# Two adaLN vectors and half a gate moved out of the routing stage of a two-layer hybrid MoE trunk, with the middle loads reordered

## What is computed

```
mod = silu(c) @ w_mod[i] + b_mod[i]                       # 6 vectors of 1024: one 1024x6144 product per layer
sh_m, sc_m, g_m, sh_f, sc_f, g_f = split(mod, 6)
h = modulate(rmsnorm(x, norm_mix[i]), sh_m, sc_m)
y = hybrid_ab(h, ...) if i == 0 else multiscale_pool(h, ...)   # sparse attention + spatial gating; or pooling
x = x + g_m * y
h = modulate(rmsnorm(x, norm_ffn[i]), sh_f, sc_f)
x = x + g_f * hier_moe(h, ...)                            # group by argmax, two of its 8 experts, SwiGLU, 32 experts of 1024x256
```

## Time and profile before

| | us |
|---|---|
| median of 3 runs | 732.48 (732.18 to 732.56) |
| the profiled execution, its own time | 732.8 |
| its span, first to last instruction | 730.7 |
| TensorE busy | 644.6 (88%) |
| VectorE busy | 372.7 (51%) |
| ScalarE busy | 172.8 (24%) |
| mean granted TensorE clock | 0.98 of full |
| moved by DMA | 269.61 MB, mean 369 GB/s |

### The profile page before, as it was taken

One profiled execution on the slowest core, in us unless ns is written; L12 is line 12 of the kernel. 1 busy time (PEld: TensorE's weight loads), 2 busy tenths in 40 slices (PEclk: granted clock), 3 DMA queues, 4 the chain that ended last, 5 costly groups with the idle time before them and its releaser, 6 DMA issues.

```text
span 730.7 us, 11411 instructions
## 1 busy us (share of the span) xinstructions
PE 644.6 (88%) x4226; PEld 388.3 (53%) x4226; DVE 372.7 (51%) x903; ACT 172.8 (24%) x368; POOL 24.9 (3%) x54
## 2 busy tenths in 40 slices
PE   2699998998998898998899899999898899898994
PEld 1487565466754454545455446675445455455542
DVE  1268868966734533344334468664344334433345
ACT  2113441030421221113111240442113211221113
POOL 5100400000000000000000000000000000000000
PEclk9999999996999999999999999899999999999998
DMA  8999535995699999999999999987999999999991
GB/s 332 352 399 398 173 116 198 409 360 213 260 420 421 421 421 422 423 422 421 422 422 423 418 398 409 375 341 303 427 418 421 422 422 423 421 421 423 422 392 57
DMA packets 49677, 269.61 MB, mean 369 GB/s; under 512 B 3796, under 2 KB 5908, under 8 KB 25072
## 3 DMA queue, kind: packets, MB, share of 16 engines
q1 hardware_dynamic: 48864, 268.22, 90.6%
q0 software_dynamic: 784, 1.00, 0.6%
HBM read 268.16 MB, written 1.05 MB: 368 GB/s over the span
## 4 chain that ended last, share of the span: by engine, by line
PE 47%; DMA 38%; DVE 5%; SPq 5%; issue 2%; ACT 1%; POOL 0%; DVEq 0%; POOLq 0%; ACTq 0%
DMA ring<-in_w_up 35%; PE bank L880 9%; PE bank L859 8%; PE bank L894 5%; PE bank L592 4%; PE bank L739 4%; DMA early_w<-in_w_in 3%; PE bank L805 2%; PE bank L664 2%; PE bank L674 2%; PE bank L522 2%; PE bank L763 1%; PE bank L847 1%; SPq L346 1%; PE bank L627 1%
## 5 line engine op out<-in xcount | busy, mean ns | idle before, releaser
L859 PE MATMUL bank<-ring,arena 128*64 128x256 f32 x1024 | 117.3, 382 | 30.3 <-DMA ring<-in_w_up 30.3
L847 PE MATMUL bank<-ring,arena 128*64 128x256 f32 x1024 | 117.6, 382 | 12.3 <-DMA ring<-in_w_gate 12.3
L1154 ACT CAST xn_parts<-arena 128x512 fp32r<-128x512 f32 x64 | 39.6, 619 | 306.0 <-DVE arena L1607 306.0
L859 PEld LDWEIGHTS bank<-ring,arena 128*64 128x64 f32 x1024 | 71.1, 137 | 75.7 <-DMA ring<-in_w_up 42.6
L880 PE MATMUL bank<-dn_w,hT 128*64 128x512 f32 x480 | 109.5, 598 | 0.0
L847 PEld LDWEIGHTS bank<-ring,arena 128*64 128x64 f32 x1024 | 81.1, 137 | 41.3 <-issue 16.5
L1582 DVE SCALAR_TENSOR_TENSOR hT<-hT,bank 128x256 f32<-128x256 f32 x32 | 19.8, 619 | 119.5 <-PE bank L859 119.5
L894 PE MATMUL bank<-xn_parts,sel 128*128 128x512 f32 x256 | 67.0, 405 | 0.0
L880 PEld LDWEIGHTS bank<-dn_w,hT 128*64 128x64 f32 x480 | 32.0, 137 | 61.6 <-issue 61.0
L1607 DVE SCALAR_TENSOR_TENSOR arena<-bank,hT,gates 128x512 f32<-128x512 f32 x64 | 47.9, 749 | 22.1 <-PE bank L880 22.0
L894 PEld LDWEIGHTS bank<-xn_parts,sel 128*128 128x128 f32 x256 | 45.8, 188 | 20.8 <-issue 12.4
(11 more groups left out here) (284 smaller groups left out, 677.4 us busy)
## 6 DMA issues: line engine op xcount, KB each, us to landing
ring<-in_w_gate SPq DMA_DIRECT2D x32, 2048.0 KB, 13.7
ring<-in_w_up SPq DMA_DIRECT2D x32, 2048.0 KB, 18.2
dn_w<-in_w_down SPq DMA_DIRECT2D x30, 2048.0 KB, 10.3
ring<-in_w_mod SPq DMA_DIRECT2D x23, 2048.0 KB, 16.4
ring<-in_w_in SPq DMA_DIRECT2D x2, 2048.0 KB, 20.7
ring<-in_w_down SPq DMA_DIRECT2D x2, 2048.0 KB, 14.6
early_w<-in_w_in SPq DMA_DIRECT2D x1, 2048.0 KB, 20.8
dn_w<-in_w_in SPq DMA_DIRECT2D x1, 2048.0 KB, 16.2
```

The lines of the kernel that those rows point to most:

```text
L847: ins = pe.matmul(bank[2][h * WIN:(h + 1) * WIN, 0:FE], xw[:, b, h, k, :], w[:, h, 0, k, :], start=(k == 0), stop=(k == KT - 1))
L859: ins = pe.matmul(bank[3][h * WIN:(h + 1) * WIN, 0:FE], xw[:, b, h, k, :], w[:, h, 1, k, :], start=(k == 0), stop=(k == KT - 1))
L1154: act.copy(xn_parts[:, 0, b, at], y_s[:, b, at]).then_inc(e["y_hi"], 1)
```

## The change

The first half of (1,0) is taken among the index scores, the second half after the keys; the first half of (0,4) is TensorE's; (1,1) is loaded to the arena and taken whole behind the logits; the second half of (0,5) is split in two steps each before and inside `route(0)`. The first expert pairs then wait for `m3b`, and for `m5a` and `out1`. The norm's row of the output is moved from the middle to `route(0)`. In the middle (1,4) goes before (1,3), and the folded shift behind the logits.

```diff
         front = [(("mod", 0), 0), (("mod", 1), 1), (("mod", 2), 2), (("mod", 3), 3), (("in", "kv"), ATT), (("in", "qi"), EARLY_W),
-                 (m2a, 0), (m2b, 1), (("in", "q"), ATT), (("in", "v"), 3), (("in", "u"), 2), (m4a, 0), (m4b, 1),
-                 (("out", 0), EARLY_W), (("out", 1), 3), (m3a, 0), (m3b, 2), (m5b, ATT), (m5a, 1), (n0a, 0), (n0b, 2), (n1a, 1), (n1b, 3)]
-        middle = [(m, slot) for m, slot in zip(halves((1, 2)) + halves((1, 3)) + halves((1, 4)) + halves((1, 5)),
-                                               (0, 1, 3, 2, 0, 1, 3, 2))]
+                 (m2a, 0), (m2b, 1), (n0a, 2), (("in", "q"), ATT), (("in", "v"), 3), (n0b, 0), (("in", "u"), 1),
+                 (("out", 0), EARLY_W), (m4a, 2), (m4b, 0), (("out", 1), 3), (m3a, 2), (m3b, 1), (m5a, 0), (m5b, ATT),
+                 (n1a, ARENA_A), (n1b, ARENA_B)]
+        middle = [(m, slot) for m, slot in zip(halves((1, 2)) + halves((1, 4)) + halves((1, 3)) + halves((1, 5)),
+                                               (1, 0, 3, 2, 0, 1, 3, 2))]
...
-                if plan[n] == m5b:
+                if slot_of(n) in (ARENA_A, ARENA_B) or plan[n] == m5b:
                     sp.wait_ge(S["p_turned"], 6)
                     sp.wait_ge(S["bT_ready"], 1)
+                    sp.wait_ge(S["pv_done"], 4)
...
-                sp.wait_ge(S["chunk_done"], chunk_no[n0b if l == 0 else ("mod", 21)] + 1)
+                if l == 0:
+                    sp.wait_ge(S["dve_used"], by_dve.index(m3b) + 1)
+                else:
+                    sp.wait_ge(S["chunk_done"], chunk_no["mod", 19] + 1)
                 gate_load(l, 0, 0)
                 up_load(l, 0, 0)
-                sp.wait_ge(S["chunk_done"], chunk_no[n1b if l == 0 else ("mod", 23)] + 1)
+                if l == 0:
+                    sp.wait_ge(S["dve_used"], by_dve.index(m5a) + 1)
+                    sp.wait_ge(S["chunk_done"], chunk_no["out", 1] + 1)
+                else:
+                    sp.wait_ge(S["chunk_done"], chunk_no["mod", 23] + 1)
                 gate_load(l, 1, 2)
                 up_load(l, 1, 2)
...   tensor engine: the gain row goes ahead of kv; then
-            head_units(range(6), qiT, kiT, (3, 4, 6), S["score_done"], S["score_relu"])
+            units = qiT, kiT, (3, 4, 6), S["score_done"], S["score_relu"]
+            head_units(range(3), *units)
+            vector((1, 0), (0,))
+            head_units(range(3, 6), *units)
...
             ins.then_inc(S["kup_done"], 1)
+            vector((1, 0), (1,))
...
             turn_p(1)
+            vector((0, 4), (0,))
...
-            project_u(1)
             turn_p(4)
             turn_p(5)
+            project_u(1)
...   tensor engine, route
                 if l == 0:
-                    turn_raw(l, (0,)), vector((1, 0), (0,)), turn_raw(l, (1,)), vector((1, 0), (1,))
+                    turn_raw(l), fold()
                 else:
-                    vector((1, 3), (1,))
-                    pe.wait_ge(S["row_kept"], 1)
-                    vector((1, 4), (0,)), turn_raw(l), vector((1, 4), (1,))
-                    pe.wait_ge(S["col_kept"], columns.index((1, 3)) - 1)
-                    norm_out_row(1, bank[0])
+                    vector((1, 4), (1,)), vector((1, 3), (0,)), turn_raw(l), vector((1, 3), (1,))
...   the logits stand here
                 if l == 0:
-                    vector((1, 1), (0,))
+                    vector((1, 1))
                 else:
+                    fold()
+                    pe.wait_ge(S["col_kept"], columns.index((1, 4)) - 1)
+                    norm_out_row(1, bank[0])
                     pe.wait_ge(S["row_kept"], 2)
                     vector((1, 5))
...   after the counting products
                 if l == 0:
-                    vector((1, 1), (1,))
+                    pe.wait_ge(S["col_kept"], columns.index((0, 3)) - 1)
+                    norm_out_row(0, bank[0])
...   scalar engine: keep_p(4), keep_p(5) now stand ahead of keep_u(1), keep_heads(1) ahead of the tanh of u
...   vector engine
-            accumulate((0, 4), (0,))
+            accumulate((0, 4), 1)
             dve.wait_ge(S["u_kept"], 2)
             gelu_poly(flat(usq), flat(uT), S["u_poly"])
+            keep_heads(1)
...
-            keep_heads(1)
-            accumulate((0, 4), (1,))
-            accumulate((0, 3), (0,))
+            accumulate((0, 3), 0)
             residual(0, 0, 3, hflat, S["mix_done"], 1)
...
             residual(0, 2, 6, hflat, S["mix_done"], 2)
+            accumulate((0, 5), 1, (0, 1))
             scale_shift(1, 0, 2)
...   route: low_parts(t) is the subtraction of L1467 for one tile
+                low_parts(0)
+                if l == 0:
+                    accumulate((0, 5), 1, (2, 3))
...   after the last product of the gates
+                low_parts(1)
                 dve.wait_ge(S["tot_done"], l + 1)
...
                 positions()
-                if l == 0:
-                    accumulate((0, 5), (1,))
...   pooling
-                for i in range(2):
-                    done(tt(y[:, i, 0:win - 1], y[:, i, 0:win - 1], edge[:, 0:win - 1], ALU.mult))
+                done(tt(y[:, :, 0:win - 1], y[:, :, 0:win - 1], edge[:, 0:win - 1].unsqueeze(1).to_broadcast([P, 2, win - 1]), ALU.mult))
```

More of the change, by code:

```diff
@@ L230, in banks_of @@
         def banks_of(vec):
-            return (0, 1) if vec in GATE else (columns.index(vec) % 2,)
+            return (2, 5) if vec == (0, 2) else (0, 1) if vec in GATE else (columns.index(vec) % 2,)
         def stage_of(vec):
@@ L246, in free_banks @@
             past = turns[:turns.index(vec)]
-            gates_past = [v for v in past if v in GATE]
+            gates_past = [v for v in past if v in GATE and v != (0, 2)]
             if gates_past:
@@ L531, in reduce @@
             def reduce(vec):
-                pe.wait_ge(S["dve_used"], 2 * BY_DVE.index(vec) + 2)
-                free_banks(pe, vec)
+                pe.wait_ge(S["dve_used"], by_dve.index(halves(vec)[1]) + 1)
+                shared = halves(vec)[0] in by_pe
+                if not shared:
+                    free_banks(pe, vec)
                 if vec in GATE:
                     for half in range(2):
-                        pe.matmul(bank[half][:, :], ones[:], vec_sum[vec][:, half * HALF:(half + 1) * HALF], start=True, stop=True
+                        pe.matmul(bank[banks_of(vec)[half]][:, :], ones[:], vec_sum[vec][:, half * HALF:(half + 1) * HALF], start=True, stop=True
                                   ).then_inc(S["gate_done"], 1)
@@ L605, in _ @@
             vector((0, 1), (1,))
+            for q in range(4):
+                ins = pe.matmul(bank[7][32 * q:32 * q + 32, 0:KT * 32].rearrange("p (k i) -> p k i", k=KT),
+                                ident[:, GAIN_ROW:GAIN_ROW + 1].to_broadcast([P, 32]), by_quadrant(rows[:, :], q, True),
+                                start=True, stop=True)
+            ins.then_inc(S["gain_row"], 1)
             w = arrived(("in", "kv"))
@@ L823, in route @@
                 rows_of((gate1, gate2), 7)
-            def norm_out_row(half, to):
-                pe.matmul(to[:, :], ident[:, OUT_ROW:OUT_ROW + 1].to_broadcast([P, P]), rows[:, half * HALF:(half + 1) * HALF],
-                          start=True, stop=True).then_inc(S["row_done"], 1)
             def experts(l):
@@ L932, in _ @@
             gate((1, 2), 0), gate((1, 2), 1)
-            vector((1, 3), (0,))
+            vector((1, 4), (0,))
             pe.wait_ge(S["hT_act"], 12)
@@ L1030, in _ @@
             keep_gate((0, 2))
-            for i, b in enumerate((5, 7)):
+            for i, b in enumerate((1, 7)):
                 if i == 0:
@@ L1264, in modulated, with accumulate @@
                     ins.then_inc(S["hT_dve"], 1)
[L1266 removed]
+            def accumulate(vec, part, steps=range(KT // 2)):
                 acc, r = vec_sum[vec], BIAS_ROW[vec]
[L1269 to L1281 removed]
+                key = halves(vec)[part]
+                if part == 0:
+                    done(ts(acc, rows[:, :], ident[:, r:r + 1], None, ALU.mult))
+                dve.wait_ge(chunk_in[slot_of(place[key])], arrivals(place[key]))
+                for kk in steps:
+                    k = part * (KT // 2) + kk
+                    w = mod_at(place[key])[:, kk, :]
+                    if kk == 0 and part == 1 and halves(vec)[0] in by_pe:
+                        ins = ts(acc, w, cs[:, 2, k:k + 1], None, ALU.mult)
+                    else:
+                        ins = stt(acc, w, cs[:, 2, k:k + 1], acc, ALU.mult, ALU.add)
+                    if kk < KT // 2 - 1:
+                        done(ins)
+                    else:
+                        ins.then_inc(S["dve_used"], 1)
+                        dve.wait_ge(S["dve_used"], by_dve.index(key) + 1)
             def residual(gate, n, b, tmp, ready, value):
```

186 lines of the change are left out of this document (92 added, 94 removed).

## The result

The changed kernel takes 724.38 us (median of 4 runs, 721.56 to 726.49) against 732.52 (732.18 to 732.67) for the kernel before on the same chip: a ratio of 0.9898 with a 95% interval of 0.9877 to 0.9919, 8.1 us faster. 7.0 were forecast, and a time of 725.5 in a range of 722.0 to 729.0. The profiled execution took 724.7 us with a span of 722.6 and a mean granted clock of 0.984. The chain and the timeline put the start of the same matmuls up to 0.35 us apart, so differences are taken within one view.

The account below looks back on a forecast made before the run. The prediction took the compute chain ahead of each expert loop's full weight stream as the bound. Its terms, +1.0 − 3.5 − 2.2 + 0.4 − 0.6 − 1.3 − 0.8 = −7.0, gave 725.5 us, range 722.0 to 729.0.

Parts of the forecast that it names:

- Step 1: Attention: three vector pieces added to TensorE, most of it regained before the output projection; +1.0 us, ends −0.5 and +3.1.
- Step 2: Output projection to last logit in layer 0: two pieces of (1,0) leave; −3.5 us, ends −3.0 and −4.15.
- Step 3: Layer 0, logits to gathers: (1,1) stands whole in the wait for VectorE's chain; −2.2 us, ends −2.5 and +0.2.
- Step 4: Gathers of layer 0: TensorE has little to do before them and may lose clock; +0.4 us, ends 0 and 1.7.
- rival (a): Clock fails twice, (1,1) at half clock throughout and 1.7 instead of 0.4 in the gathers; 729.2 us, chance 0.12.
- Step 5: Layer 0, gathers to full stream: earlier first down load gives −0.6 us, and −1.3 of backlog; ends together 0 and −2.4.
- rival (b): Head start not passed on: first units do not follow layer 1, the transfers' pause merely moves; 727.4 us, chance 0.12.
- My yardstick: Layer 0: landing of the up weights behind the second down load, whose shift reaches the program's end one to one.
- Step 6: Middle, through layer 1's routing: merged edge products −0.55, counts 0.2 to 0.8 sooner; −0.8 us, ends +1.0 and −2.0.
- rival (c): Larger gain: attention loses nothing, the middle gives 2.0, the gathers lose no clock; 722.9 us, chance 0.16.
- (d): Slower: weight chunk n0a lands late among the attention scores and holds everything behind it; 735.5 us, chance 0.03.
- (e): Vectors move but something else ended last at the same point, no change within 0.2%; 732 us, chance 0.03.

Follow-up runs that it names:

- The quarter of (1,0): Changed kernel with (1,0) computed from only two of its eight weight blocks, loads unchanged: 722.7 us, ratio 0.9873.
- the last experiment: Changed kernel with the last of the four sums of (0,5)'s second half moved behind the positions, norm row left in place: 723.29 us, ratio 0.9879.
- The experiment on the sums: Changed kernel with the second half of (0,5) summed whole behind the positions, so the first down load is late again: 726.68 us, ratio 0.992.
- the version with both edits: Changed kernel with the norm's second row taken in the pooling and the last sum of (0,5) behind the positions: 721.26 us, ratio 0.9845.
- the one with the row alone: Changed kernel with the output norm's second row taken in the pooling instead of between fold and last gate: 722.79 us, ratio 0.9865.
- after: The changed kernel itself, without further edits, against the kernel before: 724.38 us, ratio 0.9898.

## Why the prediction was right, and where its terms were off

The time (724.4 for 725.5), the sign and the mechanism hold: the work that left the path ahead of the gathers is what made the kernel faster, and the early first down load added the rest. The closeness of the sum is in part luck. Up to the full stream of layer 0 the terms came to −6.2 and the trace shows −8.7; the middle was forecast at −0.8 and lost 0.5. Two errors, of 2.5 and of 1.3 us, partly cancel. By its steps:

**Step 1, attention: +1.0 forecast, −0.04 measured.** The first values came 2.4 late (+3.1 forecast). The first piece cost less than I had: the q projection started at 62.67, 0.55 late (62.12 before) and not 1.1. The bracket of 0.59 us was not all the idle time in its place: by the timelines the score products of this stretch (L627 before, L647 after) took 5.15 us with their waits (53.84 to 58.99) and take 4.08 now, so 1.1 was there to be filled; the other two cost 1.9 together, as forecast (1.1 and 0.9). Behind the values the way back was as described: the wait at 118.81 is gone, and of the 1.71 us ahead of the output projection 0.83 is left, where I had 0.7. The +1.0 was rounded up from a sum of +0.7 out of caution for ScalarE, and no wait for ScalarE appeared. The loads were in time. The quarter of (1,0) shows that the pieces do cost: 1.8 of 2.6 us.

**Step 2, to the logits: −3.5 forecast, −5.2 measured** at the last logit (161.52 for 166.75, with the projection where it was). By the timelines the first logit came 3.6 sooner (157.34 for 160.97), inside the bounds of −3.0 to −4.15, and 1.6 came from the logits themselves: 4.18 us for 5.76, because the clock fell later in them (3.1 us after their start and not 1.4, by the granted clock of the windows). I had carried the duration of one execution over to another order of work; this is the term that was sized wrongest. Of that 0.5 went back at once: VectorE read the logits at 162.00, as it was in its two sums of (0,5) (159.14 to 161.76). I had named these sums for their load and not for what stands behind them in VectorE's list; the last experiment puts the price at 0.4 to 0.6.

**Step 3, logits to gathers: −2.2 forecast, −1.4 measured** (12.53 us from the last logit, 13.94 before); counted from VectorE's read it is 12.05, −1.9. The whole of (1,1) fitted into the wait, as worked out. That is the core of the change, and its second half put back behind the counts costs 4.4 us in its own experiment, not the 2.2 of the step: there it stands behind an idle stretch and pays twice. Steps 1 to 3 together reach the gathers at −6.64; −4.7 was forecast.

**Step 4, the clock in the gathers: +0.4 forecast.** The place was wrong: the gathers took 7.88 us and the gate came 8.77 behind their start (8.84 before). But the clock did fall, earlier, and the row product (1.65) and the slot rows (2.07, at full clock 1.08) bore it. The trace without that fall puts it at 0.7. The Trainium skill, TensorE: Matmul & The Clock Gate (Part 1: The HAM clock gate), by which the half rate is the default and activity releases it, was on the right side in this, by 0.7 us and not by the 3.7 of rival (a).

**Step 5: −0.6 and −1.3 forecast, −1.0 and −1.1 measured** (202.69 − 174.05 = 28.64 for 29.65; then −7.65 grows to −8.74). The experiment on the sums gives 1.9 for the two, as forecast. So rival (b) falls. My yardstick, the landing of the up weights, was not the place: from 204.38 they took 15.8 us and were early, and TensorE's next wait was for the third down load.

**Step 6, middle: −0.8 forecast, +0.5 in the profile.** The edge products gave what was forecast: from the start of the last residual of layer 0 to that of the last pooling products it is 17.92 us for 18.49, −0.57 (418.01 to 435.93; 426.78 to 445.27). The loss is behind that. In one trace each the new order is 0.4 us better than the old one, and by the estimate above, good to 0.5, the whole middle is 1.3 better than before's with equal clock; 1.7 us went to a longer stretch of half clock. The terms that I had named, fold, row and gate behind the logits, are the ones in the chain. What failed is the same as in step 2: durations taken as if the clock were given with the instruction.

The sum came out 1.1 too small; rival (c), more than I take, came nearest in its first part (the attention loses nothing), and (d) and (e) did not come in. What stays open: what decides at which product the clock falls, and why the version with both edits is 1.5 us under the one with the row alone when the rows show 0.4 to 0.6. They ran in different groups, and each number has about 1 us of spread. No run puts (1,0) back into `route(0)`, so step 2 is read from the trace of the whole change.

## What to carry to other kernels

Work that fills a wait is worth more than its length where the engine would else idle: half of (1,1), 1.86 us long at full clock, cost 4.4 when it was put back, since TensorE then stood idle ahead of the counts and lost its clock there. Price a piece in its old place by what stands around it after the move, and read the other engine's list at the new place, since a sum of 1.3 us that fits an idle stretch can still hold the one read that matters. And where a stage of thin products is on the path, take its duration as a range: a single profile shows one of several.

## What the runs showed of the hardware

TensorE's granted clock falls to half though the engine is 100% busy by the profile, in stretches of products of 36 columns; the same 16 products of the fold took 1.95, 2.39 and 3.61 us in three executions (the late sums, the last experiment, after; all in `route(1)`). In the same order of instructions it fell at 450.6 us, or not at all, and the stage from the last down issue of layer 0 to the counts took 68.1 or 63.5 us. That one stage can thus make most of the 6 us by which the runs of one kernel differ, with the mean clock between 0.982 and 0.989.

In `route(0)` the thirteen profiles of the changed kernel and its edits show what TensorE did before a fall at or behind the counts. In five it had waited 1.41 to 2.34 us just ahead of the counting products, and in all five the clock fell to half between 167.3 and 168.9, around these products. In six it had waited 0.57 us or less, and the clock stayed at 1.00 from the counts through the gathers. In the two of after (0.62 us) it fell at about 170.7. All six had lost clock earlier, in the logits or the first half of (1,1), and TensorE's longer work there took up the wait; four of the five had not. So a fall that was spared in the logits came back at the counts. Idle time and thin products stand together in all of these, and no run parts them.

The Trainium skill, TensorE: Matmul & The Clock Gate (Part 1: The HAM clock gate), says of the warm-up at a kernel's start that the number of matmuls in it varies between runs of one kernel; these traces show the same of falls in the middle of one. It puts the cost of that warm-up below 1% of a typical span. The spread here, 5 us of 722, is 0.7%, which is more than half of what the whole change gained.
